# Solver products issued with 32 stationary columns per tile

## What is computed

```python
for layer in range(DEPTH):
    hn = rmsnorm(x, norm_mix_g[layer])
    proj = hn @ w_in[layer]
    ...
    sol = lax.linalg.triangular_solve(eye + m, rhs, left_side=True, lower=True, unit_diagonal=True)
    ...
    x = x + merged @ w_out[layer]
    hn = rmsnorm(x, norm_ffn_g[layer])
    x = x + swiglu(...)        # layer 0;  moe_swiglu(...) in layer 1
```

## Time and profile before

| | us |
|---|---|
| device time, median of 3 runs (lowest, highest) | 2041.08 (2038.54, 2041.73) |
| span of the profiled execution, first to last instruction | 2037.5 |
| PE busy | 1961.5 (96%) |
| PEld busy | 1740.2 (85%) |
| DVE / ACT / POOL busy | 392.2 / 273.1 / 88.0 |
| instructions | 66,780 |
| mean granted TensorE clock | 0.987 of 2.4 GHz |

### The profile page before, as it was taken

One profiled execution on the slowest core, in us unless ns is written; L12 is line 12 of the kernel. 1 busy time (PEld: TensorE's weight loads), 2 busy tenths in 40 slices (PEclk: granted clock), 3 DMA queues, 4 the chain that ended last, 5 costly groups with the idle time before them and its releaser, 6 DMA issues.

```text
span 2037.5 us, 66780 instructions
## 1 busy us (share of the span) xinstructions
PE 1961.5 (96%) x31214; PEld 1740.2 (85%) x31214; DVE 392.2 (19%) x945; ACT 273.1 (13%) x580; POOL 88.0 (4%) x174
## 2 busy tenths in 40 slices
PE   7999999999999999999999799999999999999997
PEld 7888887888777688888888699999999898989897
DVE  3336331110000133533311300101000101010001
ACT  1213214000000122222310000000000000000001
POOL 4010101000000001011000000000000000000000
PEclk9899999999999999999999799999999999999999
DMA  7413123467443041311346399999999999999996
GB/s 241 124 43 104 43 69 118 145 205 249 145 145 100 25 151 58 98 49 44 116 133 223 128 347 407 407 407 407 407 407 407 407 407 407 407 407 407 407 407 267
DMA packets 214760, 482.92 MB, mean 237 GB/s; under 512 B 11582, under 2 KB 110092, under 8 KB 214668
## 3 DMA queue, kind: packets, MB, share of 16 engines
q1 hardware_dynamic: 214668, 481.54, 63.5%
HBM read 480.46 MB, written 1.05 MB: 236 GB/s over the span
## 4 chain that ended last, share of the span: by engine, by line
PE 84%; DMA 6%; SPq 4%; DVE 3%; issue 1%; ACT 1%; POOL 0%; DVEq 0%; ACTq 0%
PE bank L1193 29%; PE bank L626 19%; PE bank L1147 7%; DMA pool<-in_moe_w_down_dram 6%; PE bank L716 5%; PE bank L1074 4%; PE bank L1107 4%; SPq L2123 3%; PE bank L1090 3%; PE bank L639 2%; PE bank L680 2%; PE bank L1298 1%; SPq L2128 1%; PE bank L1037 1%; DVE pool L1817 0%
## 5 line engine op out<-in xcount | busy, mean ns | idle before, releaser
L1193 PE MATMUL bank<-pool 128*64 128x80 f32 x21504 | 759.3, 234 | 32.8 <-DMA pool<-in_moe_w_down_dram 24.1
L1193 PEld LDWEIGHTS bank<-pool 128*64 128x64 f32 x21504 | 752.6, 138 | 40.9 <-DMA pool<-in_moe_w_down_dram 26.3
L626 PE MATMUL bank<-hnT,pool 128*128 128x256 f32 x1856 | 431.5, 386 | 0.4 <-DVE pool L1879 0.4
L626 PEld LDWEIGHTS bank<-hnT,pool 128*128 128x128 f32 x1856 | 349.2, 192 | 55.9 <-issue 8.5
L1147 PEld LDWEIGHTS bank<-hnT,pool 128*128 128x128 f32 x640 | 121.6, 190 | 23.4 <-issue 7.6
L1147 PE MATMUL bank<-hnT,pool 128*128 128x256 f32 x640 | 140.7, 379 | 0.0
L2023 DVE TENSOR_TENSOR pool<-pool,bank 128x320 f32<-128x320 f32 x32 | 15.6, 488 | 638.5 <-ACT pool L1584 638.5
L716 PEld LDWEIGHTS bank<-pool 64*64 64x64 f32 x3008 | 94.8, 135 | 17.2 <-issue 11.3
L1584 ACT ACTIVATE pool<-bank 128x320 f32<-128x320 f32 x32 | 14.0, 437 | 689.3 <-PE bank L1193 689.3
L716 PE MATMUL bank<-pool 64*64 64x32 f32 (+2 forms) x3008 | 103.4, 221 | 2.6 <-DVE pool L1663 1.6
L564 POOL TENSOR_TENSOR pool<-pool,level_mask 128x256 f32<-128x256 f32 x72 | 51.8, 735 | 783.6 <-DVE pool L1739 503.5
(11 more groups left out here) (324 smaller groups left out, 1204.4 us busy)
## 6 DMA issues: line engine op xcount, KB each, us to landing
pool<-in_moe_w_up_dram SPq DMA_DIRECT2D x128, 896.0 KB, 16.6
pool<-in_moe_w_gate_dram SPq DMA_DIRECT2D x128, 896.0 KB, 16.6
pool<-in_w_in_dram SPq DMA_DIRECT2D x66, 1024.0 KB, 5.3
pool<-in_moe_w_down_dram SPq DMA_DIRECT2D x64, 1024.0 KB, 16.8
pool<-in_moe_w_down_dram SPq DMA_DIRECT2D x32, 1536.0 KB, 18.6
pool<-in_ffn_w_gate_dram SPq DMA_DIRECT2D x11, 1024.0 KB, 8.4
pool<-in_ffn_w_up_dram SPq DMA_DIRECT2D x11, 1024.0 KB, 5.4
pool<-in_ffn_w_down_dram SPq DMA_DIRECT2D x11, 1024.0 KB, 5.0
```

The costliest lines, as they stand in the source:

```text
L626: ins = mm(ps[:, s * T:(s + 1) * T], w[:, k, (j + s) * P:(j + s + 1) * P], hnT[:, k, :], start=(k == 0), stop=(k == KD - 1))
L1193: ins = mm(bank[rows, cs], w[:, rows], rhs, start=start, stop=stop, skip_group_check=True)
```

## The change

`solver` calls a new helper `strip_mm` where it called `chunk_mm`. The helper cuts each stationary operand of 64 columns into two strips of 32, and issues a product for each: the tile is 64 rows by 32 columns, and the result goes to the 32 partitions of PSUM that belong to the strip. The moving operand of both strips is the same. A pair of matrices is thus four tiles (rows 0 to 63 with columns 0 to 31 and 32 to 63, rows 64 to 127 with columns 64 to 95 and 96 to 127) where it was two. The numbers computed, the waits, the signals and the order of groups stay. The other users of `chunk_mm` keep it.

```diff
+            def strip_mm(out, lhs, rhs):
+
+                for b in range(2):
+                    rows = slice(C * b, C * b + C)
+                    for h in range(2):
+                        strip = slice(C * b + 32 * h, C * b + 32 * h + 32)
+                        ins = mm(out(strip), lhs(rows)[:, 32 * h:32 * h + 32], rhs(rows), start=True, stop=True,
+                                 skip_group_check=True)
+                return ins
...
             def solver(l, run, steps, share):
                 for g in range(2):
                     xt0_ready.wait(pe, l, 2 * run + g + 1)
                     for i in range(4):
-                        ins = chunk_mm(lambda r: B[2 + g][r, i * C:(i + 1) * C], lambda r: XX[r, g, 1, i, :],
+                        ins = strip_mm(lambda r: B[2 + g][r, i * C:(i + 1) * C], lambda r: XX[r, g, 1, i, :],
                                        lambda r: eye[r, :])
...
                         for i in range(4):
-                            ins = chunk_mm(lambda r: B[g][r, i * C:(i + 1) * C], lambda r: Ml[r, 4 * g + i, :],
+                            ins = strip_mm(lambda r: B[g][r, i * C:(i + 1) * C], lambda r: Ml[r, 4 * g + i, :],
                                            lambda r: XX[r, g, 0, i, :])
...
                             if b < 5:
-                                chunk_mm(lambda r: side(B[2 + g][r, i * C:(i + 1) * C], b, 0),
+                                strip_mm(lambda r: side(B[2 + g][r, i * C:(i + 1) * C], b, 0),
                                          lambda r: XX[r, g, 1, i, :], lambda r: side(Y[r, 4 * g + i, :], b, 0))
-                            ins = chunk_mm(lambda r: side(B[2 + g][r, (4 + i) * C:(5 + i) * C], b, 1),
+                            ins = strip_mm(lambda r: side(B[2 + g][r, (4 + i) * C:(5 + i) * C], b, 1),
                                            lambda r: Y[r, 4 * g + i, :], lambda r: side(XX[r, g, 1, i, :], b, 1))
```

## The result

| | before | after |
|---|---|---|
| device time, median of 4 runs each (lowest, highest), us | 2040.59 (2038.54, 2041.73) | 2098.62 (2095.26, 2105.94) |
| span of the profiled execution, us | 2037.5 | 2096.7 |
| MATMULs | 31,214 | 34,094 |
| mean granted TensorE clock | 0.987 | 0.972 |

The ratio is 1.0289, with a 95% interval of 1.027 to 1.0307: 58 us slower, where 23 us faster was forecast.

What follows compares the result with a forecast made beforehand. TensorE was taken to bound the solver: 4 x (0.87 + 0.05) + 0.27 = 3.95 us per run, 23.7 us over six runs, less 0.7 for joints, so 2041.1 - 23 = 2018 us; range 2012 to 2060.

Steps and rivals of the forecast that it cites:

- The bound and its place: Solver runs: a level costs 4.21 us and is TensorE's own time, so work taken off TensorE shortens the run.
- A pass in a tile costs 0.85 ns per larger operand column, and tiles run side by side: Solver bursts: plus some 4 ns; x burst pass 31 ns, 7.8 ns per MATMUL with four tiles.
- its start: Start of a y burst: first pass waits for half the weight load, an estimated 0.05 us off per level.
- The gain per level: Levels 1 to 4: x burst 1.03 us against 1.90, 0.87 us saved, plus 0.05 in the y burst.
- The 0.27 us of level 5: Level 5: ACT's copies gate the x burst, so only group 1's half gains, 0.22 us, plus 0.05 in the y burst.
- The feed, the unknown: Sequencer in x bursts: must deliver a load and a MATMUL every 7.8 ns; shortest pace seen 16.0 ns, no limit shown.
- Rival 2: Whole solver: feed limited above 16 ns per MATMUL, 2046 to 2071 us, farthest 2120; chance 0.23 with Rival 3.
- Rival 3: Transposition, y and x bursts: strips sharing rows take turns, +36 us, 2078 us; chance 0.23 together with Rival 2.
- the far price: Solver runs in Rival 2: feed at 29.7 ns per MATMUL, +13.2 us per run, 79 us, 2120 us.
- What would be late next: Levels 1 to 4: ACT's copies end 0.1 us before needed, projection step of 1.06 us covers DVE and POOL; no new wait.
- The expert stage is shifted as a whole: Expert stage: DMA share 1.00 over 860 us, but its loads move forward with everything else, so it hides nothing.
- Rival 1: Solver bursts: feed stops at 16 ns per MATMUL or a pass stays at 59 ns; 2034 to 2047 us, chance 0.12.

Runs made afterwards that it cites:

- The loop: Kernel before plus 1,024 unused load-and-MATMUL pairs of 64 by 32 tiles, as a hardware loop of 8 turns: 2045.43 us (one run) against 2040.56.
- the padded kernels: Kernel before and changed kernel, each with 8 unused long products per solver level: 2154.88 us with whole tiles, 2136.24 us with strips.
- the isolated stream: Kernel before plus 1,024 unused load-and-MATMUL pairs of 64 by 32 tiles, written out ahead of its work: 2074.52 us (one run) against 2041.17.

## Why the prediction was wrong

**The bound and its place.** Right. TensorE set the pace of the solver, and 56.1 of the 59.2 us lie in these six stretches.

**A pass in a tile costs 0.85 ns per larger operand column, and tiles run side by side.** Right in kind, somewhat off in size. An x burst of 128 takes 1.30 to 1.35 us on the timeline, so (1.30 - 0.22)/127 = 8.5 ns per MATMUL, 34 ns for a pass in a tile, against 31 forecast and 59 before. The loop has 8.6 ns over 128. y burst: (1.10 - 0.22)/63 = 14.0 ns, forecast 14.7. It is 0.05 us shorter (1.15 to 1.10), the size that was forecast for its start; but 63 x 0.7 ns is as much, so the reason given is not shown.

**The gain per level.** Right in sign, too large in size. The x burst went from 2.06 to 1.32 or 1.35 in the padded kernels, 0.71 to 0.74 us where 0.87 was forecast: the new burst has a longer pass than forecast (128 x 0.7 ns = 0.09 us), and the rest of the difference I can't place. The gain measured in the padded pair is 18.6 us, against 23; 2.7 us of waits for "issue" are still in it (2.0 at line 725, 0.7 at line 626). The 0.27 us of level 5 can't be told apart in it. Its gate is seen: in a level 5 of after, PE waited 0.21 us for ACT ahead of the x burst's second group, as forecast.

**The feed, the unknown.** This is the step that failed: the sum took a pair each 7.8 ns as deliverable and put nothing down for the arrival of instructions. The runs show one packet of 128 pairs each 3.3 to 3.8 us at best, 26 to 29 ns per pair, and pauses where the pairs at hand don't last that long. It is also the sign that the prediction named for being wrong: instructions slower than one pair in 16 ns. The chance of rivals 2 and 3 together was put at 0.23, because "no long stream of pairs is quicker than 29.7" was set against tile bounds that explain each pace. Both were true: each pace had a bound in the array, and 29 ns is also near the rate at which packets come (3.7 us for 128 pairs). What I did not ask is where the instructions come from. The page has a row for it among the queues (77 packets, 1.26 MB), and in the 30 us from 100 on the trace of before has 5 of them, one in 6 us (queue, packets, MB, share of the DMA engines):

```profile
q8 instruction: 5, 0.08, 1.3%
```

The forecast wanted 7.9 in 19.3 us (23.26 less 3.95), one in 2.4 us. The closest two in the whole trace of before begin 4.4 us apart, so nothing in it shows such a rate, and the case in which it can't be had deserved far more than the chance that it got. The section of the Trainium skill named above has the 256 instructions of a block; it was not among what I weighed.

**Rival 2.** Its mechanism and side were right, and its two prices enclosed the result: at least 2046 to 2071, and 2120 at 29.7 ns. A run takes 29.7 to 33.4 ns per MATMUL with everything in it (29.91 us for 1,008, 33.84 for 1,014): the projection steps' time counts for fetching, which the far price left out, and the store ahead holds too few pairs for the near one. As a sum over the solver: -18.6 for the array (as the padded pair has it), +52.8 idle, and so 22 for the clock, which is what remains to 56.1 and was not measured by itself. By the rule of the Trainium skill (TensorE: Matmul & The Clock Gate, "Wait — 56ns, not 53.3ns?"), start to start never below about 25 ns, it would have been 2093, near the result. That is luck: as a floor from MATMUL to MATMUL the rule doesn't hold for four tiles side by side, as the loop ran at 8.6 ns.

**What would be late next.** The prediction saw no new wait, and ACT and DVE as the nearest. Where the trace of after names ACT, at 124.52 with 0.93 us, it is the feed again: ACT's copies started on time at 123.22, one weight load ran at 123.65, and the second only at 124.53, with "issue" as its releaser.

**The expert stage is shifted as a whole.** Right. The three long stretches behind solver runs (from 298.20, 1013.40 and 1206.90 in after, the last with the experts) take 1602.1 us together, against 1600.3. It hides none of the loss either.

**Rivals 1 and 3.** Rival 1 (16 ns, no change) fell with the 8.5 ns of the bursts. Rival 3 fell with the y bursts of 1.10 us.

Left open: what the part of a packet's 3.7 us that is not its transfer (0.9 to 1.1 us) is made of, and what asks for the next packet; whether a solver written as a hardware loop, whose instructions need not come again, would keep the 18.6 us in spite of some 0.3 us more per turn, which wasn't tried; and why the clock fell behind some pauses and not behind others, and behind bursts of mixed shapes while PE was busy throughout, which was only seen. No version was faster than the kernel before.

## What to carry to other kernels

Before cutting products into smaller tiles, count instructions: work that is written out gets 256 of them per packet, here one packet in 3.3 to 3.8 us at best and in 6.5 us beside a busy DMA. If 128 pairs in a row don't last that long, PE stops once those at hand are used up (here after 159 pairs in 3.3 us beside a weight load), even where the average over two levels would do. Divide the packets of the instruction queue and the MATMULs of a stretch by its time, and look for idle time released by "issue". Finer tiles pay where the array is the bound and the instructions are either few (long moving operands beside them) or, by the isolated loop, in a loop (not tried in the solver); and tiles of different shapes are grouped, not alternated.

## What the runs showed of the hardware

- Instructions that are written out arrive in packets of 256, at best one each 3.7 us in the isolated stream (29 ns per load and MATMUL) and 3.3 us in after, 6.2 to 6.5 us with the DMA engines full. The transfer itself took 0.9 to 1.1 us in the isolated stream. 223 pairs ran before the first pause, exactly 128 after each packet.
- A hardware loop of 128 pairs is not fetched again, and ran at 8.6 ns per pair at full clock within a turn, 1.4 us from turn to turn.
- Four tiles of 64 by 32 run side by side, two on the same rows: 8.5 ns per MATMUL with 32 moving columns, 14.0 with 64.
- Each change between tiles of 64 by 64 and 64 by 32 costs about 0.12 us, and the clock fell to 0.50 behind bursts with 15 changes.
- Behind the pauses of 1.52 and 3.63 us PE ran at 1.2 GHz (a projection step in 1.80 and 2.08 us instead of 1.13), behind that of 2.21 us it did not (the next step took 1.13).
